# Rounding and subtracting a weight piece in one instruction of 2048 columns on each engine

## The reference

```
for l in range(2):                               # first block
    h = rmsnorm(x, g_mix[l]); proj = h @ w_in[l]  # 1024 x 8192
    ret = retention(rotary(q), rotary(k), v);  sb = stick_breaking(q, k, v)
    merged = sigmoid(ga) * (ret @ p_ret) + sigmoid(gb) * (sb @ p_sb)
    x = x + merged @ w_out[l]
    x = x + square(relu(rmsnorm(x) @ w_up[l])) @ w_down[l]   # 1024 x 4096 x 1024
x = rmsnorm(x, g_final)
h = rmsnorm(x); u = h @ w_in_2                    # second block, one layer
x = x + concat(pool_mixer(u), hgrn2_mixer(u)) @ w_out_2
x = x + square(relu(rmsnorm(x) @ w_up_2)) @ w_down_2
out = rmsnorm(x, final_norm_g_2)
```

## Time and profile before

| what | value |
|---|---|
| median of 3 runs | 1241.35 us (1241.04 to 1242.09) |
| profiled execution, its own time | 1243.06 us |
| its span, first to last instruction | 1241.3 us |
| PE busy | 1218.2 us, 98% |
| PEld busy | 1064.8 us, 86% |
| DVE busy | 888.7 us, 72%, 1036 instructions |
| ACT busy | 630.1 us, 51%, 823 instructions |
| POOL busy | 56.0 us, 5% |
| HBM read | 217.46 MB, 176 GB/s over the span |

### The profile page before, as it was taken

One profiled execution on the slowest core, in us unless ns is written; L12 is line 12 of the kernel. 1 busy time (PEld: TensorE's weight loads), 2 busy tenths in 40 slices (PEclk: granted clock), 3 DMA queues, 4 the chain that ended last, 5 costly groups with the idle time before them and its releaser, 6 DMA issues.

```text
span 1241.3 us, 17078 instructions
## 1 busy us (share of the span) xinstructions
PE 1218.2 (98%) x6818; PEld 1064.8 (86%) x6818; DVE 888.7 (72%) x1036; ACT 630.1 (51%) x823; POOL 56.0 (5%) x71
## 2 busy tenths in 40 slices
PE   8999999999999999999999999999989999999997
PEld 6888888889888888888888888888879997988886
DVE  5677898787666676677888777666677767766665
ACT  5455477544443444555677445343458457443342
POOL 0000120001000000000310001000010000100000
PEclk9999999999999999999999999999999999999999
DMA  7664555565556555655555565655646334655652
GB/s 249 186 191 153 164 176 186 170 198 176 190 184 200 183 179 181 188 158 153 171 169 187 171 200 172 203 180 192 219 136 196 103 103 136 204 188 185 202 186 102
DMA packets 162956, 219.33 MB, mean 177 GB/s; under 512 B 5713, under 2 KB 134225, under 8 KB 162898
## 3 DMA queue, kind: packets, MB, share of 16 engines
q1 hardware_dynamic: 162898, 218.52, 54.8%
HBM read 217.46 MB, written 1.05 MB: 176 GB/s over the span
## 4 chain that ended last, share of the span: by engine, by line
PE 71%; issue 17%; DVE 5%; ACT 4%; DMA 2%; POOL 1%; POOLq 0%; SPq 0%; DVEq 0%; ACTq 0%
PE ps L508 70%; DVE w_lo L1361 2%; ACT w_hi L925 1%; DMA raw<-in_w_in_dram 1%; PE ps L543 1%; POOL retqkv L1327 1%; DMA rope_c<-in_rope_dram 1%; ACT junk L939 0%; DMA raw<-in_w_down_dram 0%; DVE xs L1408 0%; DVE retqkv L1550 0%; DVE hT L1368 0%; DMA xs<-in_x_dram 0%; ACT hz L1126 0%; ACT htmp L1134 0%
## 5 line engine op out<-in xcount | busy, mean ns | idle before, releaser
L1361 DVE TENSOR_TENSOR w_lo<-raw,w_hi 128x1024 fp32r<-128x1024 f32 x402 | 486.2, 1252 | 86.7 <-ACT w_hi L925 86.4
L925 ACT ACTIVATE w_hi<-raw 128x1024 fp32r<-128x1024 f32 x400 | 400.4, 1052 | 180.2 <-DMA raw<-in_w_up_dram 119.9
L508 PE MATMUL ps<-hT,w_hi 128*128 128x512 f32 (+1 forms) x1952 | 426.3, 365 | 6.8 <-DVE gr L1374 3.5
L508 PEld LDWEIGHTS ps<-hT,w_hi 128*128 128x128 f32 x1952 | 339.8, 190 | 61.8 <-issue 4.3
L508 PE MATMUL ps<-w_hi,uT 128*128 128x512 f32 x768 | 244.5, 390 | 0.1
L508 PE MATMUL ps<-hT,w_lo 128*128 128x256 f32 x1696 | 239.7, 283 | 0.0
L508 PEld LDWEIGHTS ps<-hT,w_lo 128*128 128x128 f32 x1696 | 225.3, 191 | 7.0
L931 ACT ACTIVATE carry<-ps 128x512 f32<-128x512 f32 x114 | 67.9, 596 | 271.8 <-PE ps L508 271.8
L508 PEld LDWEIGHTS ps<-w_hi,uT 128*128 128x128 f32 x768 | 144.4, 188 | 30.3 <-DVE uT L1368 1.2
L508 PE MATMUL ps<-w_lo,uT 128*128 128x512 f32 x384 | 149.9, 390 | 0.0
L508 PE MATMUL ps<-w_hi,hT 128*128 128x512 f32 (+1 forms) x480 | 140.9, 374 | 2.3 <-issue 1.3
(11 more groups left out here) (202 smaller groups left out, 940.7 us busy)
## 6 DMA issues: line engine op xcount, KB each, us to landing
raw<-in_w_in_dram SPq DMA_DIRECT2D x76, 1024.0 KB, 5.6
raw<-in_w_up_dram SPq DMA_DIRECT2D x48, 1024.0 KB, 5.3
raw<-in_w_down_dram SPq DMA_DIRECT2D x48, 1024.0 KB, 4.9
raw<-in_w_out_dram SPq DMA_DIRECT2D x12, 1024.0 KB, 5.0
raw<-in_p_sb_dram SPq DMA_DIRECT2D x8, 1024.0 KB, 5.0
raw<-in_p_ret_dram SPq DMA_DIRECT2D x8, 1024.0 KB, 4.9
xs<-in_x_dram SPq DMA_DIRECT2D x2, 512.0 KB, 6.3
raw<-in_w_in_dram SPq DMA_DIRECT2D x2, 512.0 KB, 5.7
```

Source lines behind the costliest of these rows:

```text
L508: return pe.matmul(o, lhsT, rhs, start=start, stop=stop)
L925: act.activation(w_hi[:, s, half], raw[:, s, half], ACT.Copy).then_inc(hi_ready, 1)
L1361: last = dve.tensor_tensor(w_lo[:, s, half], raw[:, s, half], w_hi[:, s, half].bitcast(F32), ALU.subtract)
```

## The change

ScalarE rounds a piece in one instruction of 2048 columns, which raises `hi_ready` by two when it ends. VectorE waits for all of `hi_ready` of the piece and subtracts in one instruction of 2048 columns. The first piece keeps its halves, now through a function `convert_half`. The waits of TensorE, the semaphore counts and the order on every engine are the same.

```diff
@@ scalar block @@
                 act.wait_ge(raw_in[s], piece.count(1, SLOTS) * 16)
-                for half in HALVES:
-                    act.activation(w_hi[:, s, half], raw[:, s, half], ACT.Copy).then_inc(hi_ready, 1)
+                act.activation(w_hi[:, s, :], raw[:, s, :], ACT.Copy).then_inc(hi_ready, 2)
@@ vector block @@
-            def convert(piece, halves=(0, 1)):
+            def convert(piece):
 
                 s = piece.slot(SLOTS)
-                for n in halves:
-                    half = HALVES[n]
-                    dve.wait_ge(hi_ready, piece.count(0) * 2 + (n + 1))
-                    last = dve.tensor_tensor(w_lo[:, s, half], raw[:, s, half], w_hi[:, s, half].bitcast(F32),
-                                             ALU.subtract)
+                dve.wait_ge(hi_ready, piece.count(1) * 2)
+                dve.tensor_tensor(w_lo[:, s, :], raw[:, s, :], w_hi[:, s, :].bitcast(F32),
+                                  ALU.subtract).then_inc(lo_ready, 1)
+
+            def convert_half(piece, n):
+
+                s, half = piece.slot(SLOTS), HALVES[n]
+                dve.wait_ge(hi_ready, piece.count(0) * 2 + (n + 1))
+                last = dve.tensor_tensor(w_lo[:, s, half], raw[:, s, half], w_hi[:, s, half].bitcast(F32), ALU.subtract)
                 if n:
                     last.then_inc(lo_ready, 1)
@@ first layer, start @@
-                    convert(here, (0,))
+                    convert_half(here, 0)
                     turned_lo(mixer_norm, 0, 0)
-                    convert(here, (1,))
+                    convert_half(here, 1)
```

## The result

The changed kernel takes 1252.88 us (median of 4 runs, 1251.07 to 1254.09) against 1241.72 us (1241.04 to 1242.41): a ratio of 1.0088, with a 95% interval of 1.0075 to 1.0100. It is slower by 11.2 us between the medians. Between the profiled executions it is 9.6 us, 1252.66 against 1243.06 us of own time, with a mean granted clock of 0.998 in both. The forecast was 8.2 us and 1249.5 us.

A forecast was written before the change was run, and what follows sets the result against it. TensorE, busy 98% of the span, was taken as the bound. Delays of 2.64 (layer 0), 2.15 (layer 1) and 3.37 us (second block) sum to 8.2 us, giving 1249.5 us, range 1245.5 to 1253.5.

The forecast's parts named there:

- The price of a hand-over: Each conversion where VectorE waits for ScalarE: VectorE starts 0.85 us later, holds 0.07 us less, hands on 0.79 us later.
- VectorE's idle time behind: VectorE's waits on `w_hi` over the whole kernel: up from 86 to about 150 us.
- The heads: First pair of heads in layers 0 and 1: `rest_lo` has 0.51 us of slack, so +0.28 us in each layer.
- The second pair: Second pair of heads, layer 0 only: `rest_lo` has 0.28 us of slack, so +0.51 us.
- The rotation: Rotation in layers 0 and 1: chain from the conversion to `gr` has no slack, +0.79 us in each layer.
- The forget gates: Second block: two coupled conversions, VectorE waiting in each, make `hk` late; TensorE's idle before `hq,hk` grows by 0.98 us.
- MLP ends: Last down piece's conversion stands ahead of `us`, `usq` and `uT`, TensorE already waiting: +0.79 us at each of three ends.
- Levels: Second block's two levels: `qp` has 0.49 us of slack, so +0.30 us each, 0.60 in all.
- The mixer's end: Second block: `hg` 0.30 us later, then two pieces converted in a row ahead of `htok` add 0.71; 1.0 us in all.
- rival 1: Delays are absorbed because VectorE comes late anyway: no difference or a small gain, 1240.2 us; chance 0.12.
- rival 2: Slacks are larger by 0.3 to 0.5 us, so only places without slack count: 5.9 us, 1247.3 us; chance 0.23.
- the MLP starts: Start of the MLP: `htok` has 0.52 us of slack, so +0.27 us in layer 0 and +0.29 in layer 1.

The follow-up runs named there:

- The kernel with one instruction at the tight places: Against the kernel before: one instruction of 2048 columns on both engines for 88 pieces, halves in the MLP loops and at k = 20 to 39; 1252.99 us, ratio 1.0092.
- The kernel with one instruction in the heads: Against the kernel before: one instruction for the 22 pieces converted at k = 3 to 13 of the two first mixers, halves elsewhere; 1246.57 us, ratio 1.0031.

## Why the prediction was right, and where a size was off

- *The price of a hand-over*, 0.79 us: right. 0.85 or 0.86 later at the start, 2.28 or 2.29 us long instead of 2.35. The means, 1912 and 2313 ns, are at 1.90 and 2.28. The estimate from the Trainium skill, page "VectorE: DVE Perf Modes", section on the TRN2 errata, was 2.29 us for 2048 columns, and this trace agrees (2.28 to 2.29 where GpSimd isn't at work).
- *VectorE's idle time behind* `w_hi`: 159.4 us, forecast about 150. Its busy time fell by 16 us (forecast 12 to 15), ScalarE's by 17 (20 or rather less).
- *The heads*: the step that was mis-sized. "+0.28" for each first pair took only the last conversion before `rest_lo`. Measured 0.82 and 0.79, of which 0.38 is that conversion's and the rest is what goes round between the engines. That is 1.0 us of the sum. The second pair, forecast +0.51, has 1.07: here the hand-over was right, and what the sum didn't have is ScalarE's start 0.36 us later behind the load and 0.11 us of the load itself. It isn't the conversions before, since the kernel with the one instruction ahead of `rest_lo` alone has 1.11.
- *The rotation*, +0.79: 0.84 and 0.83, but not where I said. TensorE's idle time before `gr` didn't rise from 1.76 to 2.5, it fell to 1.40. The stall came earlier, 1.01 us before `rest_lo`, which I had put at 0.5 and held to be absorbed; the later `gr` then took over only the remainder. The chain sets the sum, and the waits along it only share it out.
- *The forget gates*, +0.98: 0.57, and 2.28 us of idle time before `hq,hk` in place of 2.7. The step that came out smaller is "the first shifts ScalarE by about 0.7": in this profile it was 0.35 against TensorE, because the load before the first of the two conversions landed 6.63 us after its issue in place of 7.13, and ScalarE took it up 0.44 us sooner (946.67 less 940.68 is 5.99, where TensorE had shifted by 6.43):

```profile
940.68 2.01 ACT L925 ACTIVATE w_hi<-raw 128x1024 fp32r<-128x1024 f32 x2 [2.32 <-DMA raw<-in_w_in_dram]
```

```profile
946.67 1.92 ACT L924 ACTIVATE w_hi<-raw 128x2048 fp32r<-128x2048 f32 x1 [1.97 <-DMA raw<-in_w_in_dram]
...
955.15 2.29 DVE L1358 TENSOR_TENSOR w_lo<-raw,w_hi 128x2048 fp32r<-128x2048 f32 x1 [1.27 <-ACT w_hi L924]
...
957.36 0.88 DVE L1730 SCALAR_TENSOR_TENSOR hk<-he,hcol,hz 128x256 f32<-128x256 f32 x2
```

  The second subtraction is 1.20 us later against TensorE (955.15 less 947.52, less 6.43), and `hk` 0.62, since its 0.43 us of idle time is gone, as forecast. With the load as in the kernel before the row would be 0.57 + 0.44 = 1.01, an estimate; the kernel with one instruction at the tight places gives 0.77 + 0.22 = 0.99 in the same way. The forecast of the hand-over was right, and the low reading is this one execution's.
- *MLP ends*: 0.80, 0.53 and 0.79 for 0.79. The 0.53 is against a first profile in which the unchanged kernel was itself 0.25 us slow in that row; against the second it is 0.78. *Levels*: 0.76 for 0.60. *The mixer's end*: 1.02 for 1.0, but its stall is before `yT` (0.41 us at 1052.57), not before `htok`, and spread over several matmuls.
- *The median*: of the 3.4 us that the forecast fell short, 1.5 are in the profile (1252.66 against 1251.2). The other 1.9 are that the kernel before has its median 1.7 us under its profiled time, which I carried over, and the changed one 0.2 us above. Runs at the same granted clock differ by less than 11.2: 1251.07 us, the changed kernel's one run at 0.999, against 1241.2, the median of 28 runs at 0.999 of the kernel before; 1253.09 against 1242.7 at 0.998 (3 and 18 runs). That is 9.9 and 10.4 us, and 9.7 in the table's rows, or some 10.1 with the load at the forget gates as before. The forecast's 8.2 us is thus about 2 us short, half of it at the first pairs of heads. Two things that the sum had no term for, ScalarE's late start and the quick load at the gates, are 0.4 us each and cancel in this one profile; that is luck, but it is small beside the terms that came out.
- *Rivals*: absorption (rival 1) fell with the table. That only places without slack count (rival 2) fell with the levels, the MLP starts and the first pairs, which had 0.5 us of slack and lost 0.3 to 0.8 us.

The page "Perfetto Trace Analysis" of the Trainium skill, section "Optimizing Scalar/DVE Operations", says that breaking instructions up may finish work sooner where these engines aren't saturated but cause bubbles on others. Between one part and two it did, by 11 us; between two and four it did not.

## What to carry to other kernels

Where one engine's result is another's operand, an instruction's length is the delay of the hand-over: merging two halves costs the second engine a half of the first, at every place where it has been waiting. Count those places by TensorE's stalls, not by idle time: here 112 of 200 merged pieces cost nothing that the runs can tell (0.7 us, up to 1.9) and 88 cost 10 to 11 us. Before you explain the difference of two single profiles in a stretch, look at how long the loads in it took: here 1.28 us less of one load moved a row by 1.19 us. Where two engines hand work to each other in turn, follow the chain over several pieces, since each late hand-over starts the next one late.

## What the hardware showed that I had not expected

**GpSimd's small operations last longer beside longer VectorE instructions.** The same four multiplications of 128x512, in the kernel before and in the changed one:

```profile
L1314 POOL TENSOR_TENSOR gr<-gr,gtmp 128x512 f32<-128x512 f32 x4 | 6.2, 1542 | 21.0 <-ACT gtmp L1065 21.0
```

```profile
L1313 POOL TENSOR_TENSOR gr<-gr,gtmp 128x512 f32<-128x512 f32 x4 | 10.8, 2709 | 18.5 <-ACT gtmp L1064 18.5
```

That is 1.17 us more each. With VectorE in halves and ScalarE in one it is 1546 ns, with VectorE in one and ScalarE in halves 2732 ns: it is VectorE's length that counts. GpSimd's busy time rose by 10.6 us, of which these four and the four of `gtmp_odd` make 9.2, and no wait of TensorE names it.

**The granted clock halves for a few microseconds after a stall, in some executions and not in others.** Windows of the kernel before in its first profile, and again in the second (columns: window, its length, busy time and instructions of PE, PEld, DVE, ACT, POOL, granted clock, DMA share, GB/s):

```profile
920.00:928.00 8.00, 5.30 (x41) 4.83 (x41) 5.41 (x10) 4.23 (x12) 3.03 (x6) 1.00 0.34 121
928.00:932.00 4.00, 4.00 (x21) 4.00 (x22) 4.00 (x4) 2.99 (x3) 0.00 (x0) 0.57 0.02 4
```

```profile
920.00:928.00 8.00, 5.21 (x40) 4.74 (x40) 5.40 (x10) 4.23 (x12) 3.03 (x6) 1.00 0.40 138
928.00:932.00 4.00, 3.51 (x29) 3.52 (x30) 4.00 (x5) 3.56 (x4) 0.00 (x0) 1.00 0.01 4
```

```profile
927.91 3.58 PE L508 MATMUL ps<-hT,w_hi 128*128 128x256 f32 x16 [1.55 <-DVE hT L1368]
```

```profile
928.49 2.17 PE L508 MATMUL ps<-hT,w_hi 128*128 128x256 f32 x16 [1.56 <-DVE hT L1368]
```

The same sixteen matmuls behind the same idle time took 3.58 us in the one, mostly at the lower level (1.2 GHz), and 2.17 us in the other at 2.4 GHz. It is the -1.49 of the row 915-935: the changed kernel has the slow stretch in the same place (granted 0.59 in its 934 to 938 us), and so it cancels in that row. The kernel with one instruction in the heads has it at another place, behind its stall on `rest_lo`:

```profile
92.00:96.00 4.00, 2.61 (x23) 2.41 (x22) 3.47 (x5) 2.40 (x2) 0.00 (x0) 1.00 0.44 111
96.00:100.00 4.00, 4.00 (x15) 3.37 (x15) 3.96 (x4) 0.84 (x1) 0.00 (x0) 0.57 0.44 170
```

which is 1.45 of its 3.00 us in the row 75-95. The stall itself is the rest: 1.54 us at the matmul on `rest_hi`, with a load of 7.65 us, 0.68 more than in the kernel before. In every trace in which I found such a stretch TensorE had idled for 1 to 3 us in the few microseconds before, but most such idle times had none behind them. A new stall can thus cost its own length or its own length and some 1.5 us; for a difference of 0.1% single profiles don't do, and runs are to be compared at the same granted clock. What decides whether the clock falls after a given stall stays open.
